# Two buffers for the convolution's input in the differential stage, and its taps dealt over 23 parts of a head instead of 20

## The reference, cut to what matters

```python
proj = h @ w_in[l]                                   # 7168 columns
q, k, v, u, g = jnp.split(proj, splits, axis=-1)     # q, k, v of 8 heads; u for the convolution; g gates
q = rms_norm(q.reshape(B, S, N_HEADS, 2, HEAD_DIM), q_norm_w[l])
k = rms_norm(k.reshape(B, S, N_HEADS, 2, HEAD_DIM), k_norm_w[l])
...
p = probs(qb1, k1f) - lamf * probs(qb2, k2f)         # two softmaxes with bias, causal, their difference
a = jnp.einsum('bhqk,bhkd->bhqd', p, vf)
a = rms_norm(a, subln_w[l]) * (1.0 - lam_init)
...
u_a, u_b = jnp.split(u, 2, axis=-1)
c = causal_depthwise_conv(u_a * jax.nn.sigmoid(u_b), conv_w[l], conv_b[l])   # 31 taps
```

## Time and profile before

| | |
|---|---|
| time, median of 3 runs (lowest to highest) | 3442.72 us (3442.67 to 3446.35) |
| the profiled execution's own time | 3441.59 us |
| its span | 3439.5 us |
| mean granted PE clock, as a share of full | 0.933 |
| busy over the span: PE, DVE, ACT, POOL | 86%, 46%, 36%, 21% |
| this stage's attention steps | from 1318.7 us to about 2200 us of the span |

### The profile page before, as it was taken

How to read it: one execution, slowest core, us unless ns; L and a number is a source line. 1 busy time by engine, 2 the same in 40 slices (tenths; PEclk the granted TensorE clock), 3 DMA queues, 4 the chain that set the end, 5 groups by cost and what they waited for, 6 DMA issues and landing times. The chain is left out here.

```text
span 3439.5 us, 35301 instructions
## 1 busy us (share of the span) xinstructions
PE 2974.0 (86%) x13448; PEld 2400.5 (70%) x13448; DVE 1580.6 (46%) x1931; ACT 1234.6 (36%) x2003; POOL 710.0 (21%) x317
## 2 busy tenths in 40 slices
PE   6999998777778769889898999694985999998998
PEld 5787886656667557667677678582775877787786
DVE  3666652356763237787777766514222220111121
ACT  3555542334531235455544555423113110111110
POOL 2111121100012112332233323212211212121111
PEclk8999999988999879999999999897998999999999
DMA  4112122132233112121211222241420111111112
GB/s 109 43 44 62 56 74 64 21 62 44 51 110 135 55 65 63 44 62 51 63 39 56 63 63 74 104 129 55 146 93 18 49 37 49 43 49 43 43 43 74
DMA packets 239268, 218.87 MB, mean 64 GB/s; under 512 B 29304, under 2 KB 200856, under 8 KB 239128
## 3 DMA queue, kind: packets, MB, share of 16 engines
q1 hardware_dynamic: 238096, 215.41, 20.6%
q10 hardware_dynamic: 1032, 1.57, 0.3%
HBM read 156.66 MB, written 41.42 MB: 58 GB/s over the span
## 5 line engine op out<-in xcount | busy, mean ns | idle before, releaser
L179 POOL TENSOR_TENSOR w_lo<-w_raw,w_hi 128x1024 fp32r<-128x1024 f32 (+3 forms) x228 | 535.2, 2349 | 2124.8 <-ACT w_hi L171 2124.8
L171 ACT ACTIVATE w_hi<-w_raw 128x1024 fp32r<-128x1024 f32 (+3 forms) x228 | 224.1, 986 | 787.6 <-PE u_y_ps L1763 222.3
L2386 DVE SCALAR_TENSOR_TENSOR d_acc<-d_padded,vectors,d_acc 128x1024 f32<-128x1024 f32 x240 | 397.3, 1655 | 4.5
L197 PE MATMUL d_pp<-h_hi,w_hi 128*128 128x512 f32 x896 | 367.7, 410 | 12.3 <-PEq L67 5.2
L197 PE MATMUL d_pp<-h_hi,w_lo 128*128 128x512 f32 x896 | 368.3, 411 | 0.0
L197 PE MATMUL d_pp<-h_lo,w_hi 128*128 128x512 f32 x896 | 365.3, 408 | 0.0
L197 PE MATMUL s_pp<-h_hi,w_hi 128*128 128x512 f32 x512 | 206.8, 404 | 11.9 <-PEq L67 11.9
L197 PEld LDWEIGHTS d_pp<-h_hi,w_hi 128*128 128x128 f32 x896 | 174.6, 195 | 56.3 <-issue 18.0
L2170 POOL TENSOR_TENSOR d_probs<-d_probs 128x128 f32<-128x128 f32 (+3 forms) x64 | 123.5, 1929 | 410.7 <-ACT d_probs L2284 410.6
L197 PE MATMUL s_pp<-h_hi,w_lo 128*128 128x512 f32 x512 | 205.4, 401 | 0.0
L197 PE MATMUL s_pp<-h_lo,w_hi 128*128 128x512 f32 x512 | 204.6, 400 | 0.0
(11 more groups left out here) (333 smaller groups left out, 6511.3 us busy)
## 6 DMA issues: line engine op xcount, KB each, us to landing
w_raw<-in_w_in SPq DMA_DIRECT2D x97, 512.0 KB, 4.0
w_raw<-in_w_gate_up SPq DMA_DIRECT2D x44, 512.0 KB, 3.9
w_raw<-in_w_down SPq DMA_DIRECT2D x22, 512.0 KB, 3.7
gates<-s_gate SPq DMA_DIRECT2D x16, 512.0 KB, 5.2
f_gate<-gates SPq DMA_DIRECT2D x16, 512.0 KB, 5.2
w_raw<-in_w_out SPq DMA_DIRECT2D x16, 512.0 KB, 3.8
w_raw<-in_w_proj SPq DMA_DIRECT2D x16, 512.0 KB, 4.7
x_tok_in<-in_x SPq DMA_DIRECT2D x8, 512.0 KB, 7.4
```

The source lines that it names most:

```text
L171: act.activation(self.hi[:, s, 0:chunks, :], self.raw[:, s, 0:chunks, :], ACT.Copy).then_inc(self.rounded[s], 1)
L179: pool.tensor_tensor(self.lo[:, s, 0:chunks, :], self.raw[:, s, 0:chunks, :], f32(self.hi[:, s, 0:chunks, :]), ALU.subtract).then_inc(self ...
L197: mm = pe.matmul(halves(ps)[h], w[:, k, :], x[:, k, h * HALF:(h + 1) * HALF], start=(k == 0 and r == 0), stop=(k == chunks - 1 and r == 2))
L2386: dve.scalar_tensor_tensor(out=acc[:, :], in0=x, scalar=wt, in1=acc[:, :], op0=ALU.mult, op1=ALU.add).then_inc(c["taps"], 1)
```

## The change

The change has four parts.

- `d_padded` gets two buffers, by the parity of the head. `feed_conv` of head h waits for the taps of head h - 2 instead of h - 1. To make room, `d_raw` has two slots instead of three: v shares the slot of k (v of head 0, which comes before k of head 0 is used up, goes to `d_o_sb`). ACT's copy of v therefore waits for `low_k`, its copy of k for the turned v, and its first copy to `d_o_sb` for the turned v of head 0.
- The taps of head h now end at part 16, one part after the second `feed_conv` of head h + 1, and those of head h + 1 begin at part 17. They lie in 23 parts.
- They are dealt in proportion to the room in each part, by new estimates of the load, with at most about two in a part. In a part x = 0 an odd tap goes to the first half, in the others to the second.
- SP's store of `d_acc` moves one weight tile later in SP's list.

```diff
-        raw = mem.sb("d_raw", [P, 3, TOK])
+        raw = mem.sb("d_raw", [P, 2, TOK])
...
-        padded = mem.sb("d_padded", [P, PAD + TOK])
+        padded = mem.sb("d_padded", [P, 2, PAD + TOK])
...
+        v_raw = [o_sb] + [raw[:, 1, :]] * LAST
...
-        conv_end = [part_of[stream.index(("a", h)), 0] - 2 for h in range(1, HEADS)] + [PARTS * (STEPS - 1)]
+        conv_end = [at + 1 for at in conv_in_at[1:]] + [PARTS * (STEPS - 1) + 1]
...
-            room = range(conv_in_at[h] + 1, conv_end[h] + 1)
+            room = range(conv_in_at[h] + (2 if h else 1), conv_end[h] + 1)
             n = CONV - (TAPS_FIRST if h == 0 else 0)
-            time, other = [sum(f(at) for at in room) for f in (pe_load, dve_load)]
-            share = (other + TAP * n) / time
-            done, t, o = 0, 0.0, 0.0
-            for at in room:
-                t, o = t + pe_load(at), o + dve_load(at)
-                upto = n if at == room[-1] else min(n, max(done, int((share * t - o) / TAP)))
+            room_for = [0.4] * len(room)
+            share = 0.6
+            while sum(room_for) < TAP * n:
+                share += 0.01
+                room_for = [min(max(share * pe_work(at) - dve_work(at), 0.3), 2.2 * TAP) for at in room]
+            total, done = 0.0, 0
+            for at, x in zip(room, room_for):
+                total += x
+                upto = n if at == room[-1] else round(n * total / sum(room_for))
                 taps_in[at] = (h, CONV - n + done, CONV - n + upto)
                 done = upto
...
-            conv_after = {tile_at(conv_end[h]): h for h in range(LAST)}
+            conv_after = {tile_at(conv_end[h] + 1): h for h in range(LAST)}
...
                         if what == "k":
                             act.wait_ge(c["k_low"], 2 * n)
+                            act.wait_ge(c["v_turned"], 2 * n)
                         if what == "v":
-                            act.wait_ge(c["v_turned"], 2 * n)
+                            act.wait_ge(c["k_low"], 2 * n + 2)
...
-            def taps(at, lo, hi):
+            def taps(at, first_half):
 
                 if at in taps_in:
                     h, x, y = taps_in[at]
-                    for t in range(x + (y - x) * lo // 4, x + (y - x) * hi // 4):
+                    middle = x + (y - x + (at % PARTS == 0)) // 2
+                    for t in range(x, middle) if first_half else range(middle, y):
                         tap(h, t)
...
-                    if h:
-                        dve.wait_ge(c["taps"], CONV * h)
+                    if h >= 2:
+                        dve.wait_ge(c["taps"], CONV * (h - 1))
```

More of the change, by code:

```diff
@@ L2071, in differential_and_conv @@
-        V_TURN, Q_SQUARE, O_SQUARE, K_SQUARE = 4, 5, 6, 8
+            if x == 0:
+                load += 0.5 + (1.15 + 0.28 * (b + 1) if b < 4 else 0.8 + 0.285 * (b + 1))
+                load += 0.15 + 0.135 * (min(4, b) if b else 4)
+            if x == 2 and (b == 0 or b > 4):
+                load += 0.15 + 0.135 * (b - 4 if b else 4)
+            return load
         taps_in = {}
         for h in range(HEADS):
-            room = range(conv_in_at[h] + 1, conv_end[h] + 1)
+            room = range(conv_in_at[h] + (2 if h else 1), conv_end[h] + 1)
```

34 lines of the change are left out of this document (20 added, 14 removed).

## The result

The changed kernel takes 3425.2 us in the median of 6 runs (3416.53 to 3430.05), the kernel before 3443.26 us beside it (3441.05 to 3446.35). The ratio is 0.994, with a 95% interval of 0.9925 to 0.9954: faster by 0.6%, 18.1 us. The forecast was 3426 us. The profiled execution took 3416.88 us, its span 3414.8 us, with a mean granted PE clock of 0.940. It is one of the two fastest of the six (3416.53 and 3416.88, the other four 3424.61 to 3430.05), so what its profile shows is a gain somewhat above that of the median.

The account below looks back on a forecast made before the run. DVE and PE wait for each other, so DVE's round through a head, work plus waits, was taken as the bound. Terms -5.7 - 4 - 4 - 3 = -16.7 us from 3441.59 gave 3424.9, forecast as 3426 us; range 3388 to 3454.

Parts of the forecast that it names:

- The pacer: Heads 1 to 4: the length of DVE's own round counts, about 86.4 us of work and 25.0 of waits.
- Step 2: Heads 1 to 4: three taps behind `normalise` of o instead of two, from 14.62 to 15.9 us; ACT's chain decides.
- Heads 1 to 4: DVE's steps sum to 109.5 us against a mean of 111.4; half the difference to head 1 gives -4 us.
- Head 0: Six taps fewer save 9.9 us of DVE's time, less the store's wait and uncovered exponentials: -5.7 us.
- the store and the exponentials: Head 0, against the saved taps: 2.9 us waiting for the store and 1.3 for step 7's less covered exponentials.
- Head 5: Still 34 taps but no run of six; PE's 12.3 us idle, less the store's wait and DVE's work: -4 us.
- Head 6: PE idle for only 3.9 us; three more taps lie in DVE's 33.8 us of waits: -3 us.
- The store's wait: At tap 0 in seven heads, DVE waits for `d_acc` to be stored: 2.9 us, bounds 2.3 and 8.7.
- The long wait of the earlier trace: Rival: SP reaches the store late, as where it took 9.0 us; seven heads pay 6.1 more, 3469 us; chance 0.12.
- the rival by which the gains and the new wait cancel: A store's wait of 4 to 5 us, or half of head 0's gain, gives 3436 to 3449 us; chance 0.20.
- PE's waits: The 7.02 us stop goes; idle spreads, 3 to 5 us each at steps 4, 5, 6 and 0; second `feed_conv` late.
- More meetings with POOL: Rival: spread taps meet POOL's instructions on the shared port more, five heads pay 10.6 us each, 3479 us; chance 0.06.

Follow-up runs that it names:

- e7: e4 plus a rule moving one tap from part x = 1 to an empty part x = 0, under ACT's exponentials: 3398.34 us, ratio 0.9859.
- e5: The changed kernel with taps over 64 columns instead of 1024, most of the convolution left out: 3340.31 us, ratio 0.9694.
- e11: The changed kernel with 7 taps of head 0 ahead of the attention instead of 13, so head 0 has 33 again: 3435.49 us, ratio 0.9979.
- e1: The changed kernel with SP storing another tensor than the accumulator, so tap 0 need not wait for the store: 3415.65 us, ratio 0.9921.
- e4: The changed kernel with the next head's taps beginning one part later, at part 18: 3410.44 us, ratio 0.9911.
- e2: The kernel before with the new dealing alone: one input buffer, three raw slots, the old 20 parts: 3415.72 us, ratio 0.9922.
- e6: The changed kernel with POOL adding 16 columns of the two maps instead of all: 3407.9 us, ratio 0.9894.
- e3: The changed kernel with the old dealing formula and halves, so the buffers alone: 3480.6 us, ratio 1.0113 against the kernel before.
- e12: e2 (one buffer, three raw slots, no tap in step 4) plus the placing edits of e7 and e9: 3380.02 us, ratio 0.9823.
- e9: e7 with the second half of a part's taps ahead of `normalise` in parts 5, 7 and 9: 3391.21 us, ratio 0.9851.

## Why the prediction was right, point by point

**The pacer.** The prediction's main step was to count the length of DVE's round, its work and its waits, step by step. Every step of head 1 came out within 0.84 us, and the sum within 0.3 us, the latter with the luck that steps 0 and 2 missed in opposite directions. Step 2 was forecast short for a reason: the prediction let one of its two new taps vanish in a wait for ACT's chain, but the two together cost 2.1 us, and e7 shows that the place to hide one was under the exponentials. e5 shows the rest of it: with short taps a head falls to 96.5 to 98 us and PE stops hardly any more. That DVE paces heads 1 to 4 is shown.

**Heads 1 to 4.** Forecast -4 us, measured -6.2. The head lengths after lie within 0.1 us of each other, so the extra time by which the mean of heads 1 to 4 had stood above head 1 (111.4 to 109.6) went whole, not by half. The term was mis-sized by 2.2 us.

**Head 0.** Forecast -5.7, measured -6.15. e11 puts the six taps back and pays 8.3 us for them, the store's wait being in both, where the prediction had 9.9. With 33 taps head 0 of e11 is 2.1 us longer than before, where the prediction had 4.2 for the store and the exponentials. Both terms were too large, and the errors nearly cancelled.

**Head 5.** Forecast -4, measured -9.8: mis-sized. DVE's busy time in this window fell from 96.67 us to 88.59 at nearly the same number of instructions (98 and 99), most of it in the taps, 60.25 to 52.70 us. The prediction had counted PE's stall and not that the taps would meet POOL less. That DVE paces this head too is argued: in e1, where the same taps take 57.4 us, the head is 117.6 us long.

**Head 6.** Forecast -3, measured +4.0: the sign was wrong. The step that failed is "its three more taps lie in DVE's 33.8 us of waits". They didn't all: DVE's waits there were 33.8 us and are 35.5, with three more taps and the store's wait. PE's idle time rose from 3.9 to 5.7 us and its busy time by 2.2. The clock in this window was 0.96, against 0.99 in the earlier trace rows; that it follows from the stops is argued, not shown. Heads 5 and 6 together came to -5.8 where -7 was forecast, so the two errors nearly cancelled, and that was luck. In e1 and e11, with the same taps in these heads, the two take 233.5 and 233.7 us, 1 us less than before. Why head 6 of the same dealing takes 115.2 us in one execution and 119.8 in another (e11) is open.

**The sum.** The terms gave -16.7 us; the windows gave -18.1, the stage 19.2 less in the profiled execution, the medians 18.1 less. The forecast is good to 2 us, and part of that is the cancelling in heads 0, 5 and 6.

**The store's wait.** Forecast 2.9 us in seven heads, 20 in all; measured 16.3, 1.7 to 2.7 each. From the end of the 31st tap to the landing it is 2.68 to 4.26 us. The long wait of the earlier trace rows did not come back, and the rival with it fell. Its price is about 11 us in heads 0 to 4 (e1); of the whole kernel it is 6 to 10 us, as said there. With it fell the rival by which the gains and the new wait cancel.

**PE's waits.** As forecast, the 7.02 us stop is gone, and the stops are spread: up to 4.3 us for `feed_conv` at step 5, 3.3 for exponentials, 1.8 for `low_t`. They are shorter than the 3 to 5 us each that were forecast: in head 1 it is 3.25, 1.98, 1.09 and 1.79 us. The prediction named the late second `feed_conv`. It did not price it as a loss of its own, and e4 and e2, with 16.1 and 1.5 us of that wait and heads 1 to 4 of the same length, show no loss from it.

**More meetings with POOL.** That rival fell too: the mean of a tap went from 1.655 us to 1.617. The mechanism is there, though: a tap of 1.28 us alone takes up to 3.3 beside POOL, and e6 turned 20 us less of such meetings into 17 us of time. By the rule of the Trainium skill ("SBUF — State Buffer", "SBUF: two separate sides"), one of the two waits for the other's whole instruction; the trace agrees. In e1 `w_lo` begins while the second of the two taps shown above still runs, until 1938.98:

```profile
1937.85 3.37 POOL L179 TENSOR_TENSOR w_lo<-w_raw,w_hi 128x1024 fp32r<-128x1024 f32 x1
```

It takes 1.04 us more than the shortest `w_lo` of this shape (2.33), about the 1.1 us that the tap ran on. The next tap begins at 1939.10 and takes 3.21 us, 1.9 above the median, about the 2.1 us that `w_lo` ran on.

**What was not seen.** That the change's two halves have opposite signs, and that they do not add. The dealing alone is worth some 27 us, the buffers alone cost some 38, and both together gave 18: on top of the new dealing the second buffer cost some 9 us between medians, not 38. The prediction costed the buffer at nothing but for the store. In heads 1 to 4 under the new dealing that was nearly right, by e4 and e2. Under the old dealing it was wrong: the steps of e3 show the taps that come into step 4 paid in full, and little saved elsewhere (1.3 us in step 3). What counts is how many taps lie where they are paid, steps 4 and 5 above all. In the table the taps in steps 4 to 7 go with the head's length: 19 taps with about 117 us, 15 with 107 to 111, 14 and 12 with 106 to 108, and, with a tap under the exponentials, 14 with 104 and 12 with 101.5. It is an order, not a law: the store's wait moves with it, and e2 and e4 have the same length with 12 and 14 taps.

**Open.** The variation of heads 5 and 6 between executions; how much of the store's wait they give back; and whether two buffers or one is the better with the best placing, since e12 and e9 differ by 2.2 us a head in heads 1 to 4 and not clearly in their times.

## What to carry to other kernels

Where two engines wait for each other by turns through lists that are fixed, add up one engine's round, work and waits, step by step, and ask of each piece of filler work which wait it lies under: the same tap costs nothing under a chain of another engine and its full time, or more, ahead of what that other engine needs next. A second buffer that lets filler work go on at more places is worth something only if those places are waits. Here they were not: with two buffers heads 1 to 4 were at best as long as with one (e4 and e2), and 2.2 us longer once taps were moved under waits (e9 and e12). When a change has two parts, time each alone before you keep both, and don't expect their effects to add.
